# Query norms moved into the softmax's scale and the delta rule's output norm, in a two-block transformer kernel

## The chip, the cores and the metric
One core of one Trainium2 chip runs the whole program in one launch. The metric is the device time in microseconds. Three timed runs of the kernel before gave 3331.95, 3326.08 and 3330.05 us, median 3330.05. TensorE (PE) multiplies, VectorE (DVE), ScalarE (ACT) and GpSimd (POOL) work elementwise, SyncE (SP) issues the transfers.

## The reference
Two transformer blocks over 512 tokens of width 1024, in fp32. Block one is a SwiGLU layer, three mixers in parallel (retention, differential attention, attention to a memory of 256 rows) and a second SwiGLU layer. Block two is a gated delta rule beside an mLSTM, a feed-forward layer, a sliding-window attention and a second feed-forward layer. What the change touches:

```python
# differential attention: 8 heads, two maps each, width 64
dq = _rope_partial(_rms(dq.reshape(B, S, DIFF_HEADS, 2, DIFF_DK), diff_q_norm[l]), d_cos, d_sin)
dk = _rope_partial(_rms(dk.reshape(B, S, DIFF_HEADS, 2, DIFF_DK), diff_k_norm[l]), d_cos, d_sin)
s = einsum('bhrqd,bhrkd->bhrqk', q, k) / sqrt(DIFF_DK);  p = softmax(s);  a = p[0] - lam * p[1]
# memory attention: 4 heads, width 256
mq = _rms(mq.reshape(B, S, MEM_HEADS, MEM_DH), mem_q_norm[l])
mk = _rms(mk.reshape(B, M, MEM_HEADS, MEM_DH), mem_k_norm[l])
p = softmax(einsum('bshd,bmhd->bhsm', mq, mk) / sqrt(MEM_DH))
# delta rule: 4 heads, width 128; its output is linear in q
qa = l2norm(silu(conv(...))) * (A_DK ** -0.5);  ka = l2norm(silu(conv(...)))
oa = rmsnorm(gated_delta_rule(qa, ka, va, g, beta), norm_a) * silu(z)
```

## The kernel before, in words
Activations lie transposed in SBUF, channels on the 128 partitions, the 512 tokens along the free side. All weights come in 1002 panels of four 128x128 blocks. SyncE loads a panel into RAW, ScalarE rounds it to the fp32r tile WH, POOL subtracts (WL = RAW - WH). A product of a block is three matmuls, high x high, low x high and high x low (`mm3`, called by `lin` and `row_of`), each 128x512.

The program is one list of steps, `PLAN`, built by `plan_ffn`, `plan_ret`, `plan_diff`, `plan_mem`, `plan_ab`, `plan_swa` and `plan_feed`. Each engine's function walks the same list from front to back and issues, for every step, its own part (`tensor`, `vector`, `scalar`, `gpsimd`, `sync`), with semaphore waits (`at`) for what the others produce (`up`). So the order on every engine is the order of the list, and an instruction that waits holds back everything behind it on its engine. At each step ScalarE and POOL first convert the weight panels that are due (`starts`), at most six ahead. A PSUM bank is handed out by `bank`, which takes the one whose last content is consumed at the earliest step.

A norm has these parts. ScalarE squares. TensorE sums over the partitions with a column of ones (`columns`, products of one column). VectorE adds epsilon (`variance`), POOL takes the power -1/2 (`power`), VectorE sharpens it with three small operations (`factor`; `pre` is a further scaling). Since the tokens lie along the free side, TensorE must spread the factor: `spread` transposes a broadcast column with four 128x128 transposes (`turned`, line 548), and VectorE multiplies the tile by the result in PSUM.

Differential attention, head h, while head n = h+1 is prepared: `d_q(n,0)` and `d_q(n,1)` compute q and k, `d_v(n)` v, the sums for the norms of q and k (four columns) and their factor. VectorE copies the factors to two wide tiles (line 1312), `d_n(n)` turns them, four transposes for q and four for k, and VectorE multiplies. `d_rope` rotates: a matmul with a swap matrix, VectorE times sine, POOL times cosine, VectorE adds both. `d_sc(h,q)` is the scores of query block q (VectorE: mask, maximum, times -1/8; ScalarE: Exp with scale 1/8), `d_sm(h,q)` the division and the difference, `d_turn(h,q)` the transposes of the result on TensorE, `d_pv` the product with v, `d_t1` and `d_t2` the head's output norm. In the list, `d_q(n,0)` stands ahead of `d_sm(h,0)` and `d_turn(h,0)`, and `d_v(n)` ahead of `d_sm(h,3)` and `d_turn(h,3)`. `wide` products (gates, the retention's output, memory queries) fill the places between.

Memory attention: `mq(m)` queries, `mkl`/`mk` keys, `nqm` and `nkm` their norms, `mqn(h)` and `mkn(h)` the spreading, `ms` the scores and softmax, `mt` the transposes.

Delta rule, heads in two pairs: `c(h,j)` the convolution of q, k, v and Silu, `f(h)` the norms of q and k in one go (two columns), `n(h)` spread and multiply both, `dec` the decays, `LT` and `at` the products with k and q, `l` the seven levels of a triangular inverse, `uw`, `s` and `o` the recurrence and output, `z` the gate and the output norm's sum and factor, `fin` its spreading. The mLSTM's steps (`m_*`) lie in between.

Of the kernel before, what the change touches and what calls it, by code (L numbers as in the profile page):

```python
# [11 lines left out]
ACT = mybir.ActivationFunctionType  # L12
AX = mybir.AxisListType.X

T = 512
# [108 lines left out]
VOFF = {}  # L124
# [88 lines left out]
def plan_diff():  # L213
# [3 lines left out]
    p = [("d_q", 0, 0), ("d_q", 0, 1), ("d_v", 0), ("d_vt", 0), wide.pop(0), ("d_n", 0), wide.pop(0), ("d_rope", 0, 0), ("d_rope", 0, 1),  # L217
# [17 lines left out]
def plan_mem():  # L235
    p = [("mload",)] + [("mg", 1, m) for m in range(8)]
    p += [("mp", m) for m in range(5)] + [("mq", 6)] + [("mp", m) for m in (5, 6, 7)] + [("mq", 7)]
    p += [("mkl", 0), ("nqm",), ("fac", "nmem"), ("mkl", 1), ("bc", "nmem"), ("mk", 0), ("mk", 1), ("mqn", 0)]
    for m in range(2, 8):
        p += [("mkl", m), ("mk", m)] + ([("mqn", m // 2)] if m % 2 else [])  # L240
# [113 lines left out]
PLAN = plan()  # L354
# [9 lines left out]
def program(nc, x_in, mem_in, p_in, pos1, pos2, lam_in, vec_in, cst_in, dm_in, wst, out, total, dry=False):  # L364
    blocks = []
    with ExitStack() as ctx:
# [57 lines left out]
        for h_ in range(4):  # L424
            NORM["nr", h_] = ("b", 1 / 512, 4, 4, 1, 1.0)
            NORM["nqk", h_] = ("e", 1.0, 2, 4, 2, 1.0)
            NORM["no", h_] = ("e", 1 / 128, 1, 4, 1, 1.0)
            NORM["nml", h_] = ("e", 1 / 128, 1, 4, 1, 1.0)
# [12 lines left out]
        def nr(n):  # L441
            return nw(n)[:, 3, :].rearrange("p (t c) -> p t c", t=NORM[n][3])

# [13 lines left out]
        def tensor(e):  # L457
# [103 lines left out]
            for marks.step, (kind, *i) in enumerate(PLAN):  # L561
# [92 lines left out]
                elif kind == "d_v":  # L654
                    h = i[0]
                    lin(("d_v", h), ("d_v", h), "w_in", 0, cc(O_DV + 128 * h), range(8))
                    o = bank("var", ("nd", h))
# [8 lines left out]
                elif kind == "d_n":  # L666
                    h = i[0]
                    for j in range(2):
                        e.wait_ge(*at("d_wide", h, j))
                        turned(("d_normed", h, j), ("d_n", h, j), lambda t: quarter(tmp(2 + j), t))  # L670
                elif kind == "d_rope":
                    h, j = i
                    o = bank("d_sin", h, j)
                    e.wait_ge(*at("d_normed", h, j))
                    mm(o, CST[:, C_SWD:C_SWD + 128], ar(2 * (h % 2) + j), True, True).then_inc(*up("mm", "d_rope", h, j))
                elif kind == "d_sc":
                    h, q = i
                    nk = 128 * (q + 1)
                    for r in range(2):
                        o, lo = bank("d_exp", h, q, r), 64 * r  # L680
                        if q == 0 and r == 0:
                            e.wait_ge(*at("d_roped", h, 1))
# [56 lines left out]
                elif kind == "mqn":  # L739
                    spread("nqm", ("mq_normed", i[0], 1), ("mqn", i[0]), i[0])  # L740
# [7 lines left out]
                elif kind == "ms":  # L748
                    h, q = i
                    o = bank("ms_exp", h, q)[:, 0:256]  # L750
                    if q == 0:
                        e.wait_ge(*at("mk_normed", h, 1))
# [62 lines left out]
                elif kind == "f":  # L815
                    h = i[0]
                    o = bank("var", ("nqk", h))
                    e.wait_ge(*at("c_square", h, 1))
                    columns(o, 0, tmp(2), one1, True)
                    columns(o, 1, tmp(3), one1, False).then_inc(*up("mm", "fac", ("nqk", h)))  # L820
                elif kind == "n":
                    for j in range(2):
                        spread(("nqk", i[0]), ("qk_normed", i[0], j), ("n", i[0], j), j)
# [8 lines left out]
                elif kind == "LT":  # L832
                    h = i[0]
                    o = bank("kk", h)
                    e.wait_ge(*at("qk_normed", h, 1))
                    for t in range(4):
                        z = mm(quarter(o, t), quarter(slot(h, "k"), t), quarter(slot(h, "k"), t), True, True)
                    z.then_inc(*up("mm", "kk", h))
                    turned(("LT", h), ("beta", h), lambda t: SC[:, 0, 4 * t + h:4 * t + h + 1].to_broadcast([128, 128]))
                elif kind == "at":  # L840
                    h = i[0]
                    o = bank("att", h)
                    for t in range(4):
                        z = mm(quarter(o, t), quarter(slot(h, "k"), t), quarter(slot(h, "q"), t), True, True)
                    z.then_inc(*up("mm", "kq", h))
                    turned(("kd", h), ("k_turned", h), lambda t: quarter(slot(h, "k"), t))
                    e.wait_ge(*at("c_act", h, 2))
                    turned(("vb", h), ("v_turned", h), lambda t: quarter(slot(h, "v"), t))
                elif kind == "l":
# [12 lines left out]
                    else:  # L862
                        e.wait_ge(*at("l_x", h, lv))
                        e.wait_ge(*at("U", h, lv - 1))
                        if lv < 6:
                            o = bank("T", h, lv)
                            for t in range(4):
                                z = mm(quarter(o, t), quarter(U_, t), quarter(X_, t), True, True)
# [1554 lines left out]
```

## Time and profile before

| | |
|---|---|
| timed runs | 3326.08, 3330.05, 3331.95 us |
| profiled execution, its own time | 3324.88 us |
| its span (first to last instruction) | 3323.1 us |
| mean granted TensorE clock | 0.986 |
| VectorE busy | 1214.4 us (37%), 2152 instructions |
| ScalarE busy | 1230.6 us (37%), 2217 |
| POOL busy | 1743.3 us (52%), 1347 |

Busy time counts an engine's instructions in the span. A matmul's end is modelled, so back-to-back matmuls overlap. The differential attention lies between about 772 and 1160 us, the memory attention between 1160 and 1330, the delta rule and mLSTM between 1836 and 2210.

### The profile page before, as it was taken

The page shows a single profiled execution, that of the slowest core. Times are in us where ns is not written, and L with a number is a line of the kernel's source. Part 1 is how long each engine was busy: PE and PEld are TensorE (multiplying, and loading weights), DVE is VectorE, ACT ScalarE, POOL GpSimd, SP SyncE. Part 2 cuts the span into 40 slices and gives each one's busy share as a digit, 9 for nine tenths or more (in the row PEclk, how much of TensorE's full clock was granted, in tenths as well). Part 3 has the DMA queues.
Part 4 walks back from the last instruction along what each step waited for, and adds up shares of the span by engine and source line. Part 5 has one row for each costly group of instructions (what it writes and reads, how often), then busy time and mean ns, then how long its engine had stood idle before and what let it go on. Part 6 is the DMA issues. An engine that isn't in the chain of part 4 may idle for free.

```text
span 3323.1 us, 40114 instructions
## 1 busy us (share of the span) xinstructions
PE 3203.2 (96%) x15078; PEld 2612.8 (79%) x15078; DVE 1214.4 (37%) x2152; ACT 1230.6 (37%) x2217; POOL 1743.3 (52%) x1347
## 2 busy tenths in 40 slices
PE   8999999999999999999999898999999988999999
PEld 7888887777777787788888787877888776778887
DVE  4222322124555434223224655524111457341115
ACT  4332333333444435333224323234333345543333
POOL 6555655455554464465556213246555652475555
PEclk9999999999999999999999999999999999999999
DMA  4333222222222233333333102112333321223332
GB/s 163 98 92 101 86 86 76 83 82 77 64 61 61 70 106 97 88 98 98 98 96 95 54 26 58 39 54 80 101 96 95 96 70 39 64 85 100 96 101 86
DMA packets 149839, 275.58 MB, mean 83 GB/s; under 512 B 16528, under 2 KB 17808, under 8 KB 149520
## 3 DMA queue, kind: packets, MB, share of 16 engines
q1 hardware_dynamic: 149648, 273.02, 28.2%
q8 instruction: 122, 2.00, 0.2%
q14 instruction: 69, 0.57, 0.1%
HBM read 270.86 MB, written 2.10 MB: 82 GB/s over the span
## 4 chain that ended last, share of the span: by engine, by line
PE 85%; DVE 9%; POOL 3%; ACT 2%; issue 2%; DMA 0%; DVEq 0%; SPq 0%; ACTq 0%; POOLq 0%
PE PS L481 83%; PE PS L548 2%; POOL SM L2180 1%; DVE AR L1070 1%; POOL WL L2180 1%; DVE TMP L1070 1%; DVE ACC L1076 1%; DVE X L1070 1%; DVE AL L1070 1%; DVE HL L1076 1%; ACT AR L1795 1%; DVE SM L1070 1%; DVE TMP L1076 1%; DVE SM L1755 1%; DVE AR L1076 1%
## 5 line engine op out<-in xcount | busy, mean ns | idle before, releaser
L2180 POOL TENSOR_TENSOR WL<-RAW,WH 128x512 fp32r<-128x512 f32 x1002 | 1305.2, 1314 | 995.0 <-ACT WH L1795 994.2
L1795 ACT ACTIVATE WH<-RAW 128x512 fp32r<-128x512 f32 x1002 | 619.1, 627 | 1068.6 <-PE PS L481 1015.7
L481 PE MATMUL PS<-HH,WH 128*128 128x512 f32 x2296 | 914.0, 398 | 10.4 <-ACT WH L1795 7.1
L481 PE MATMUL PS<-HL,WH 128*128 128x512 f32 x2296 | 902.3, 393 | 7.9 <-DVE HL L1076 6.3
L481 PE MATMUL PS<-HH,WL 128*128 128x512 f32 x2296 | 901.5, 393 | 2.3 <-POOL WL L2180 2.3
L481 PE MATMUL PS<-AH,WH 128*128 128x512 f32 (+1 forms) x1504 | 584.3, 388 | 5.1 <-ACT AH L1795 3.5
L481 PE MATMUL PS<-AL,WH 128*128 128x512 f32 (+1 forms) x1504 | 582.1, 387 | 1.7 <-DVE AL L1070 1.1
L481 PE MATMUL PS<-AH,WL 128*128 128x512 f32 (+1 forms) x1504 | 580.9, 386 | 2.0 <-POOL WL L2180 2.0
L481 PEld LDWEIGHTS PS<-HL,WH 128*128 128x128 f32 x2296 | 435.7, 190 | 104.0 <-DVE HL L1076 12.1
L481 PEld LDWEIGHTS PS<-HH,WH 128*128 128x128 f32 x2296 | 435.3, 190 | 103.9 <-ACT WH L1795 7.4
L481 PEld LDWEIGHTS PS<-HH,WL 128*128 128x128 f32 x2296 | 434.8, 189 | 95.9 <-POOL WL L2180 4.2
L481 PEld LDWEIGHTS PS<-AL,WH 128*128 128x128 f32 x1504 | 284.2, 189 | 64.0 <-DVE AL L1070 7.9
L481 PEld LDWEIGHTS PS<-AH,WH 128*128 128x128 f32 x1504 | 284.2, 189 | 63.5 <-issue 5.5
L481 PEld LDWEIGHTS PS<-AH,WL 128*128 128x128 f32 x1504 | 284.2, 189 | 58.6 <-POOL WL L2180 2.8
L2180 POOL TENSOR_TENSOR AL<-TMP,AH 128x512 fp32r<-128x512 f32 x132 | 175.7, 1338 | 231.1 <-ACT AH L1795 231.1
L1070 DVE TENSOR_TENSOR TMP<-PS,RBT 128x512 f32<-128x512 f32 x141 | 96.8, 690 | 492.9 <-PE PS L481 487.7
L481 PE MATMUL PS<-AR 128*128 128x128 f32 (+8 forms) x1304 | 238.2, 359 | 17.0 <-DVE AR L1070 8.7
L481 PEld LDWEIGHTS PS<-AR 128*128 128x128 f32 (+2 forms) x1304 | 171.2, 192 | 74.1 <-issue 49.0
L1070 DVE TENSOR_TENSOR ACC<-ACC,PS 128x512 f32<-128x512 f32 x136 | 93.4, 687 | 266.3 <-PE PS L481 266.3
L2180 POOL TENSOR_TENSOR TMP<-TMP 128x512 f32<-128x512 f32 (+1 forms) x88 | 119.6, 1359 | 90.6 <-ACT TMP L1795 89.3
L2180 POOL TENSOR_TENSOR SM<-SM,VC 128x4 f32<-128x4 f32 (+3 forms) x47 | 67.4, 1433 | 178.0 <-DVE SM L1073 178.0
L1795 ACT ACTIVATE TMP<-TMP 128x512 f32<-128x512 f32 x132 | 82.7, 626 | 179.3 <-DVE TMP L1076 133.9
(208 smaller groups left out, 2576.0 us busy)
## 6 DMA issues: line engine op xcount, KB each, us to landing
RAW<-in_wst SPq DMA_DIRECT2D x1002, 256.0 KB, 2.6
X<-in_x SPq DMA_DIRECT2D x8, 256.0 KB, 5.0
TMP<-in_p SPq DMA_DIRECT2D x8, 256.0 KB, 3.2
out<-X SPq DMA_DIRECT2D x8, 256.0 KB, 2.0
AR<-in_dm SPq DMA_DIRECT2D x1, 1024.0 KB, 5.3
AR<-in_mem SPq DMA_DIRECT2D x1, 1024.0 KB, 5.8
CST<-in_cst SPq DMA_DIRECT2D x1, 964.0 KB, 7.6
AR<-in_pos SPq DMA_DIRECT2D x2, 256.0 KB, 2.9
```

The source lines that it names most:

```text
L481: return e.matmul(o, l, r, start=a, stop=z, skip_group_check=True)
L548: z = e.transpose(quarter(o, t), src(t), ident)
L1070: return e.tensor_tensor(o, a, b, op)
L1076: return e.scalar_tensor_tensor(out=o, in0=a, scalar=s, in1=b, op0=op0, op1=op1)
L1755: e.reduce_max(st[:, 0, :], p, AX).then_inc(*up("s_max", n))
L1795: return e.activation(o, a, f, **kw)
L2180: return e.tensor_tensor(o, a, b, op)
```

## The change
- Differential attention: q is no longer multiplied by its factor. The gain alone is multiplied in (`d_gain`, directly behind `d_q(n,0)`, after the square), and the factor times 1/8 (`eighth`) becomes Exp's scale and the maximum's multiplier. `d_n` spreads k only. The rotation's sine part stays in PSUM and is added from there.
- Memory attention: `mqn` goes. The factor of q times 1/16 (`mem_scale`) becomes the softmax's scale; the two gains are multiplied and applied to the keys.
- Delta rule: q stays as it is. Its factor times 128^-0.5 (`q_scale`) enters the output norm twice, in the variance and in the factor. The joint norm of q and k becomes two, `fk` and `fq`, one after the other.
- `split` cuts the steps of the list into finer ones, and `turns` gives an engine its own order by a table of shifts, `LATE`, which is empty.
- `d_rope(0,0)` of the first head moves ahead of a wide product and of `d_n(0)`.

```diff
-    p = [("d_q", 0, 0), ("d_q", 0, 1), ("d_v", 0), ("d_vt", 0), wide.pop(0), ("d_n", 0), wide.pop(0), ("d_rope", 0, 0), ("d_rope", 0, 1),
+    p = [("d_q", 0, 0), ("d_q", 0, 1), ("d_v", 0), ("d_vt", 0), ("d_rope", 0, 0), wide.pop(0), ("d_n", 0), wide.pop(0), ("d_rope", 0, 1),
...
-        p += [("mkl", m), ("mk", m)] + ([("mqn", m // 2)] if m % 2 else [])
+        p += [("mkl", m), ("mk", m)]
...
-PLAN = plan()
+def split(steps):
+
+    out = []
+    for s in steps:
+        kind, *i = s
+        h = i[0] if i else None
+        if kind == "fac":
+            out += [s, ("x", h)]
+        elif kind in ("nqm", "nkm"):
+            out += [s, ("x", kind)]
+        elif kind == "d_v":
+            out += [s, ("d_f", h), ("x", ("nd", h)), ("d_wide", h)]
+        elif kind == "d_q" and i[1] == 0:
+            out += [s, ("d_gain", h)]
+        elif kind == "f":
+            out += [("fk", h), ("x", ("nk", h)), ("fq", h), ("x", ("nq", h))]
...
+        elif kind == "z":
+            out += [s, ("zf", h), ("x", ("no", h))]
...
+        elif kind == "d_rope":
+            out += [s, ("d_add", *i)]
...
+PLAN = split(plan())
+LATE = {"vector": {}, "scalar": {}, "gpsimd": {}}
+
+
+def turns(engine):
+
+
+    place = {s: n + LATE[engine][s] + math.copysign(0.5, LATE[engine][s]) if s in LATE[engine] else n for n, s in enumerate(PLAN)}
+    return sorted((p, n, s) for n, (s, p) in enumerate(place.items()))
...
# TensorE
-                    for j in range(2):
-                        e.wait_ge(*at("d_wide", h, j))
-                        turned(("d_normed", h, j), ("d_n", h, j), lambda t: quarter(tmp(2 + j), t))
+                    e.wait_ge(*at("d_wide", h))
+                    turned(("d_normed", h), ("d_n", h), lambda t: quarter(tmp(3), t))
...
-                elif kind == "mqn":
-                    spread("nqm", ("mq_normed", i[0], 1), ("mqn", i[0]), i[0])
...
-                    e.wait_ge(*at("c_square", h, 1))
-                    columns(o, 0, tmp(2), one1, True)
-                    columns(o, 1, tmp(3), one1, False).then_inc(*up("mm", "fac", ("nqk", h)))
+                elif kind in ("fk", "fq"):
+                    n = ("n" + kind[1], i[0])
+                    o = bank("var", n)
+                    e.wait_ge(*at("c_square", i[0], int(kind == "fk")))
+                    columns(o, 0, tmp(2 + int(kind == "fk")), one1, True).then_inc(*up("mm", "fac", n))
                 elif kind == "n":
-                    for j in range(2):
-                        spread(("nqk", i[0]), ("qk_normed", i[0], j), ("n", i[0], j), j)
+                    spread(("nk", i[0]), ("k_normed", i[0]), ("n", i[0]))
...
# VectorE
+                    if n == "nqm":
+                        e.wait_ge(*at("factor", n))
+                        ts(mem_scale, nr(n), 0.0625, None, MUL).then_inc(*up("mem_scale"))
+                    elif n[0] == "nq":
+                        e.wait_ge(*at("factor", n))
+                        ts(q_scale(n[1]), nr(n), 128.0 ** -0.5, None, MUL).then_inc(*up("q_scale", n[1]))
...
-                    for j in range(2):
-                        src = nr(("nd", h))[:, :, 2 * j:2 * j + 2].unsqueeze(3).to_broadcast([128, 4, 2, 64])
-                        e.tensor_copy(tmp(2 + j).rearrange("p (a b c) -> p a b c", a=4, b=2), src).then_inc(*up("d_wide", h, j))
+                    src = nr(("nd", h))[:, :, 2:4].unsqueeze(3).to_broadcast([128, 4, 2, 64])
+                    e.tensor_copy(tmp(3).rearrange("p (a b c) -> p a b c", a=4, b=2), src).then_inc(*up("d_wide", h))
+                    ts(eighth(h), nr(("nd", h))[:, :, 0:2], 0.125, None, MUL).then_inc(*up("d_eighth", h))
+                elif kind == "d_gain":
+                    q = ar(2 * (i[0] % 2))
+                    e.wait_ge(*at("d_square", i[0], 0))
+                    ts(q, q, vcol("dq"), None, MUL).then_inc(*up("d_gain", i[0]))
...
-                    tt(r, psum("d_sin", h, j), tab(3), MUL).then_inc(*up("d_sin", h, j))
+                    tt(r, r, tab(3), MUL).then_inc(*up("d_sin", h, j))
+                elif kind == "d_add":
+                    h, j = i
+                    q, r, s = tmp(2 + j), psum("d_roped", h, j), ar(2 * (h % 2) + j)
...
-                    ts(st[:, 1:2], st[:, 0:1], -0.0625, None, MUL).then_inc(*up("ms_neg", h, q))
+                    e.wait_ge(*at("mem_scale"))
+                    stt(st[:, 1:2], st[:, 0:1], -1.0, mem_scale[:, q, h:h + 1], MUL, MUL).then_inc(*up("ms_neg", h, q))
...
-                    for j, p in enumerate(("q", "k")):
-                        e.wait_ge(*at("mm", "n", h, j))
-                        e.wait_ge(*at("c_square", h, j))
-                        stt(slot(h, p), slot(h, p), (128.0 ** -0.5, 1.0)[j], psum("qk_normed", h, j), MUL,
-                            MUL).then_inc(*up("qk_normed", h, j))
+                    o = slot(h, "k")
+                    e.wait_ge(*at("mm", "n", h))
+                    e.wait_ge(*at("c_square", h, 1))
+                    tt(o, o, psum("k_normed", h), MUL).then_inc(*up("k_normed", h))
...
-                    variance(("no", h))
-                    factor(("no", h))
+                elif kind == "zf":
+                    e.wait_ge(*at("q_scale", i[0]))
+                    scaled_variance(("no", i[0]), q_scale(i[0]))
...
# ScalarE
-                        act(ar(16 + 2 * (q % 2) + r)[:, 0:nk], psum("d_exp", h, q, r)[:, 0:nk], ACT.Exp, st[:, 2 + r:3 + r], 0.125,
-                            st[:, 4 + r:5 + r]).then_inc(*up("d_exp", h, q, r))
+                        act(ar(16 + 2 * (q % 2) + r)[:, 0:nk], psum("d_exp", h, q, r)[:, 0:nk], ACT.Exp, st[:, 2 + r:3 + r],
+                            eighth(h)[:, q, r:r + 1], st[:, 4 + r:5 + r]).then_inc(*up("d_exp", h, q, r))
```

## Rows read from the trace of the kernel before

**Rows 1.** The page: busy us (share of the span) x instructions of each engine
```profile
PE 3203.2 (96%) x15078; PEld 2612.8 (79%) x15078; DVE 1214.4 (37%) x2152; ACT 1230.6 (37%) x2217; POOL 1743.3 (52%) x1347
```
**Rows 2.** Groups by line and shape: busy us, mean ns, idle before and its releasers
```profile
L548 PE MATMUL PS<-CST,TMP 128*128 128x128 f32 x128 | 18.4, 276 | 0.5 <-DVE TMP L1312 0.5
```
**Rows 3.** Who waited for whom: us in total, times, longest us
```profile
PE PS L548 <- DVE AR L1076: 15.6, 12, 2.1
```
**Rows 4.** Timeline, PE, head 0: start us, us, instruction, count, idle before
```profile
832.42 1.04 PE L548 MATMUL PS<-CST,TMP 128*128 128x128 f32 x8
834.60 2.39 PE L481 MATMUL PS<-AR 128*128 128x512 f32 x8 [1.14 <-ACT AR L1795]
```
**Rows 5.** Timeline of four engines around d_turn of head 6, block 0
```profile
1079.08 0.69 DVE L1070 TENSOR_TENSOR AR<-PS,RBT 128x512 f32<-128x512 f32 x1 [2.11 <-PE PS L481]
1080.01 0.75 DVE L1073 TENSOR_SCALAR AR<-AR,SM 128x128 f32<-128x128 f32 x1
...
1079.80 0.63 ACT L1795 ACTIVATE TMP<-AR 128x512 f32<-128x512 f32 x1 [1.20 <-DVE AR L1070]
...
1078.17 2.51 POOL L2180 TENSOR_TENSOR WL<-RAW,WH 128x512 fp32r<-128x512 f32 x2 [3.50 <-ACT WH L1795]
...
1081.28 0.33 PE L548 MATMUL PS<-CST,AR 128*128 128x128 f32 x1 [0.96 <-DVE AR L1076]
```
**Rows 6.** Timeline, VectorE and PE around d_turn of head 6, block 3
```profile
1101.67 0.76 DVE L1312 COPY TMP<-SM 128x512 f32<-128x512 f32 x2
1102.67 0.48 DVE L1073 TENSOR_SCALAR AR<-AR,SM 128x512 f32<-128x512 f32 x1
...
1104.07 0.66 PE L548 MATMUL PS<-CST,AR 128*128 128x128 f32 x4 [2.07 <-DVE AR L1076]
```
**Rows 7.** Timeline, VectorE and PE at the rotation of head 1
```profile
840.08 1.51 DVE L1070 TENSOR_TENSOR AR<-TMP 128x512 f32<-128x512 f32 x1
...
841.74 0.49 PE L481 MATMUL PS<-AR 64*128 64x128 f32 x4 [0.30 <-DVE AR L1070]
```
**Rows 8.** Timeline, PE, d_n of the first head
```profile
789.38 1.09 PE L548 MATMUL PS<-CST,TMP 128*128 128x128 f32 x8 [0.46 <-DVE TMP L1312]
```
**Rows 9.** Timeline: PE in the memory attention; an activation with a tile's bias
```profile
1235.03 1.34 PE L548 MATMUL PS<-CST,SM 128*128 128x128 f32 x6 [3.03 <-DVE SM L1076]
...
1284.80 0.44 PE L548 MATMUL PS<-CST,AR 128*128 128x128 f32 x2 [0.27 <-DVE AR L1073]
...
1072.11 0.72 ACT L1795 ACTIVATE AR<-AR,VC 128x512 f32<-128x512 f32 x1 [2.53 <-DVE AR L1070]
```
**Rows 10.** Timeline at the norms of delta rule heads 0 and 1
```profile
1829.40 1.01 POOL L2180 TENSOR_TENSOR SM<-SM,VC 128x4 f32<-128x4 f32 x1 [2.83 <-DVE SM L1073]
1864.87 1.63 POOL L2180 TENSOR_TENSOR SM<-SM,VC 128x8 f32<-128x8 f32 x1 [5.88 <-DVE SM L1073]
...
1866.74 2.40 DVE L1076 SCALAR_TENSOR_TENSOR SM<-SM 128x8 f32<-128x8 f32 x2
...
1869.19 1.97 PE L548 MATMUL PS<-CST,SM 128*128 128x128 f32 x8 [5.77 <-DVE SM L1076]
...
1911.90 2.05 PE L481 MATMUL PS<-AR,TMP 128*128 128x128 f32 x8 [2.96 <-DVE TMP L1070]
```
**Rows 11.** Timeline, PE at heads 2 and 3; the group of VectorE's short products
```profile
2029.86 0.49 PE L481 MATMUL PS<-AR 128*128 128x128 f32 x2 [2.91 <-DVE AR L1070]
...
2047.66 1.94 PE L548 MATMUL PS<-CST,SM 128*128 128x128 f32 x8 [4.39 <-issue]
...
L1076 DVE SCALAR_TENSOR_TENSOR SM<-SM 128x4 f32<-128x4 f32 x68 | 15.3, 225 | 2.3
```
**Rows 12.** Busy us (x) of PE, PEld, DVE, ACT, POOL by stretch; then PE's clock, DMA
```profile
770.00:1200.00 430.00, 408.70 (x1963) 317.79 (x1962) 215.41 (x522) 179.15 (x360) 223.65 (x166) 1.00 0.24 71
...
1866.80:1873.50 6.70, 4.31 (x14) 3.76 (x15) 5.89 (x9) 1.09 (x3) 2.31 (x2) 0.50 0.29 78
...
2044.30:2051.00 6.70, 3.34 (x16) 3.37 (x17) 2.82 (x8) 0.63 (x1) 1.63 (x1) 0.50 0.00 0
```

More of the change, by code:

```diff
@@ L442, in nr, with eighth, q_scale @@
             return nw(n)[:, 3, :].rearrange("p (t c) -> p t c", t=NORM[n][3])
+        mem_gain = small("c", "mem_gain", 2)
+        mem_scale = small("c", "mem_scale", 16).rearrange("p (t c) -> p t c", t=4)
+        def eighth(h):
+            return small("b", ("d_eighth", h % 2), 8).rearrange("p (t c) -> p t c", t=4)
+        def q_scale(h):
+            return small("e", ("q_scale", h), 4).rearrange("p (t c) -> p t c", c=1)
         def sq(n, k):
@@ L1036, in tensor @@
                 elif kind == "st":
-                    n = i[0]
+                    n, q = i
                     e.wait_ge(*at("s_p", n))
-                    for q in range(2):
-                        turned(("s_turned", n, q), ("st", n, q), lambda t: s_p(n)[:, 2 * q + t // 2, 128 * (t % 2):128 * (t % 2) + 128])
+                    turned(("s_turned", n, q), ("st", n, q), lambda t: s_p(n)[:, 2 * q + t // 2, 128 * (t % 2):128 * (t % 2) + 128])
                 elif kind == "sp":
@@ L1138, in vector @@
             e.wait_ge(*at("vec"))
-            for marks.step, (kind, *i) in enumerate(PLAN):
+            for marks.step, _, (kind, *i) in turns("vector"):
                 if kind == "fac":
@@ L1264, in vector @@
                     variance(("nr", i[0]))
-                    factor(("nr", i[0]))
                 elif kind == "r_fin":
@@ L1356, in vector @@
                     variance(("nt", i[0]))
-                    factor(("nt", i[0]))
                 elif kind == "d_t2":
@@ L1656, in vector @@
                     scaled_variance(("nml", i[0]), dn[:, 0])
-                    factor(("nml", i[0]), dn[:, 0])
                 elif kind == "m_fin":
@@ L1808, in scalar @@
             e.wait_ge(*at("vec"))
-            for s, (kind, *i) in enumerate(PLAN):
-                marks.step = s
+            for marks.step, s, (kind, *i) in turns("scalar"):
                 if kind == "f_open" and i[0] == 0:
@@ L2196, in gpsimd @@
             e.wait_ge(*at("vec"))
-            for s, (kind, *i) in enumerate(PLAN):
-                marks.step = s
+            for marks.step, s, (kind, *i) in turns("gpsimd"):
                 while panels < starts(s):
@@ L2242, in gpsimd @@
                     h, j = i
-                    e.wait_ge(*at("d_normed", h, j))
-                    e.wait_ge(*(at("mm", "fac", ("nd", h)) if j == 0 else at("mm", "d_n", h, 1)))
+                    e.wait_ge(*at(("d_gain", "d_normed")[j], h))
+                    if j == 0 and h:
+                        e.wait_ge(*at("d_roped", h - 1, 0))
                     if h == 0 and j == 0:
                         e.wait_ge(*at("table", 0, 3))
-                    tt(tmp(4 - 2 * j), ar(2 * (h % 2) + j), tab(2), MUL).then_inc(*up("d_cos", h, j))
+                    tt(tmp(2 + j), ar(2 * (h % 2) + j), tab(2), MUL).then_inc(*up("d_cos", h, j))
                 elif kind == "d_t2":
```

179 lines of the change are left out of this document (114 added, 65 removed).

## The prediction

> **What bounds the kernel now.** The page's busy line comes first: TensorE (PE) is busy for 3203.2 of 3323.1 us [rows 1]. So an instruction removed on another engine is worth nothing by itself. The time moves when TensorE issues less, or when it waits less. The groups by line say what it issues: product passes of the weight panels, which the change doesn't touch, and small transposes, of which it removes some (L548 is `turned`; 128 of them read TMP) [rows 2]. The list of waits says where TensorE stands: the largest entry is transposes that wait for a VectorE result in AR, 15.6 us in 12 waits [rows 3]. The reader is to see that the idle time, 120 us, is made of pieces of 0.3 to 6 us with different releasers, so each edit is priced at its own piece, in the timeline.
>
> **The sum is made against the profiled execution**, 3324.9 us, span 3323.1 and 1.8 around it. It is 5.2 us under the median of the three timed runs, 3330.05; the sum's difference is added to that median.
>
> **Transposes removed.** Eight in a row take 1.04 us [rows 4], the last one 0.28 [rows 2]: (1.04 - 0.28) / 7 = 0.11 us each. The differential attention loses 4 in each of 8 heads (`d_n` of q), the memory attention 16 (`mqn`), the delta rule 4 in each of 4 heads (`n` of q): 32 x 0.11 = -3.5, 16 x 0.11 = -1.8, and 16 whose worth is taken up below, since they stand beside waits.
>
> **Given back at once.** In heads 0, 2 and 4 `d_pv` follows `d_n` directly and already waits for ScalarE's copy of the last turned block, 1.14 us at 834.60 [rows 4]. Four transposes fewer is 0.44 us more waiting, 3 x 0.44 = +1.3.
>
> **The new gain instruction, the dearest edit.** `d_gain(n)` comes behind `d_q(n,0)` on VectorE, waits there for ScalarE's square of the same tile, and multiplies 128x512 in place. Queued behind it on VectorE is `d_sm(h,0)`, and TensorE's `d_turn(h,0)` waits for that already, 0.96 us at 1081.28 [rows 5]. There is no cover. `d_q`'s product runs from 1079.08 to 1079.77, the square from 1079.80 to 1080.43, POOL's subtraction until 1080.68 [rows 5], so the gain starts near 1080.5 and takes 0.48 us, as the scalar product of 128x512 at 1102.67 did [rows 6]. `d_sm`'s first step, which began as `d_q`'s product ended, begins near 1081.1, 1.4 us late. Part comes back: its 128x128 product at 1080.01 took 0.75 us, more than the larger one at 1102.67, because POOL was at work [rows 5, 6]; now it runs after POOL is done. Worked through, the probabilities are late by 0.93 us here and in three heads like it, 1.0 in two where that product was slowed less, and 1.25 in head 0, where it was not slowed: 7 heads (the eighth issues no next query), +7.0. Bounds: the bare 0.48 each, +3.4, if the square were always there; no return at all, 1.4 each, +9.8. I take +7.0, as the order on the three engines is the same in all heads.
>
> **The rest of this section.** `d_turn(h,3)` waits 2.07 us in heads 1, 3, 5 and 6 for a VectorE queue that holds the factor and two wide copies (0.76 us for both) [rows 6]; one copy goes (-0.34) and a product of 8 columns comes (0.1 to 0.2): 4 x -0.2 = -0.8. The rotation's sum now reads PSUM and one SBUF tile, not two SBUF tiles. At 840.08 it took 1.51 us, and `d_sc` waited 0.30 us for it at 841.74 [rows 7]; a sum or product with a PSUM operand takes 0.69 (1079.08) [rows 5]. 2 heads x -0.3 = -0.6; in the others wide products cover it. The Trainium skill, "SBUF — State Buffer", section on who interferes with whom, has an exclusive lock between VectorE and GpSimd, which a VectorE instruction with two SBUF inputs or in a two-port mode contends for; the trace agrees at 1080.01 and 840.08, and the rule also speaks against the change, for the gain is such an instruction: where it met a whole POOL instruction it would cost up to 1.3 us more. In head 0 the move of `d_rope(0,0)` ahead of `d_n(0)` puts a rotation's matmul in front of a 0.46 us wait (789.38) [rows 8]: -0.6 with the pipeline's refill. No DMA moves, and no weight panel: the new steps consume none, so the order of conversions is kept on ScalarE, POOL and SP. Sum: -3.5 +1.3 +7.0 -0.8 -0.6 -0.6 = +2.8.
>
> **Memory attention.** -1.8 from the transposes. The wait of 3.03 us at 1235.03 stands behind two factors in a row on VectorE [rows 9]; the new `mem_scale` comes between them, +0.3. The softmax is a ring over TensorE, VectorE and ScalarE with no slack: a wait of 0.27 us already stands before its first transpose, at 1284.80 [rows 9]. An Exp with its scale read from a tile is shown nowhere; the nearest rows are an activation with a bias from a tile, 0.72 us, and one without, 0.63 [rows 5, 9], so 0 to 0.1 per step; the bias here comes from a tile already, so I take 0.03, 16 x 0.03 = +0.5 (0 to +1.6). Sum -1.0.
>
> **Delta rule.** The key's norm and the query's norm are now two roundtrips to POOL, and VectorE is blocked in both.
> - Heads 0, 1: `n(0)` stands 5.77 us for the factor at 1869.19. The key's factor alone comes near 1866.6: POOL 1.01 us for four columns (1829.40) in place of 1.63 for eight (1864.87), and three short products [rows 10]. That releases TensorE 2.5 us earlier. But VectorE is next late: it holds back the following convolution until the query's factor is done too, and POOL starts its weight subtraction right behind the power, where two short products took 2.40 us (1866.74) [rows 10]. I get 1870.4 for that convolution, +1.3, and +1.2 behind the second pair, less 2 x 0.6 for the product of q that goes and the slack VectorE had between. The wait at 1911.90, 2.96 us for VectorE [rows 10], hands this on: -0.3 in all, from -2.5 (all the earliness stays) to +1.5.
> - Head 2: TensorE waits until 2029.86 for a VectorE sum queued behind the factor [rows 11]: the second roundtrip adds 1.5. Head 3: it waits 4.39 us, until 2047.66, for the factor itself; that comes 0.65 earlier, and four of eight transposes (1.94 us) go [rows 11]: -1.6.
> - Output norm of head 3: two instructions more in front of the power and one behind it, 0.2 each as a short product has [rows 11], and nothing but four transposes beside them: +0.6.
> Sum +0.2.
>
> **Total** +2.8 -1.0 +0.2 = +2.0: 3326.9 for an execution like the profiled one, 3332.1 as a median. The finer steps move nothing by themselves: they issue the same instructions in the same order on each engine, since the table of shifts is empty.
>
> **Rivals.**
> 1. *The delta rule gives back speed too (faster).* From 1867 to 1873.5 TensorE has the lower clock, 0.50 or 1.2 GHz, around the long wait, and again from 2044.3 to 2051 [rows 12]. If the shorter waits at 1869 and 2047 leave the clock at 2.4 GHz, 4.3 and 3.3 us of work (busy in these rows) shrink by half, -2.2 and -1.7; with the 2.5 us at 1869 kept, 1.6 at 2047, 0.9 of transposes in heads 1 and 2, against +0.6, that is -8.3, and with the other two sections 3323.6. For it: the lower clock stands around such waits. Against: the wait at 1911.90 shows VectorE late there anyway.
> 2. *The longer waits in the attention drop the clock (slower).* At `d_turn(h,0)` there are transposes, short products and 0.96 us of wait together, and the wait doubles. The clock is 1.00 from 770 to 1200, with the four 2.07 us waits in it [rows 12]. A stretch as long as the one at 1867, were it full of work, costs 3.3. One fall changes nothing that could be told; from two on, +2.0 +6.6, it is slower: 3338.7, and 3345 with four. The Trainium skill, "TensorE: Matmul & The Clock Gate", Part 1, says that idleness halves the clock; by that rule the falls at 1867 and 2044 are no surprise, but the 2.07 us waits passed without one.
> 3. *The change costs nothing where I see its price*: the gain is hidden, +7.0 becomes 0, and 3325.1 results. Against it: 0.03 us lie between the product and the square that waits for it [rows 5].
>
> **Chances.** Forecast 0.58, rival 1 0.16, rival 2 0.15, rival 3 0.06, and 0.05 for what no row shows. About 0.2% (6.7 us) is what a measurement of this kernel can tell from no change. Of the forecast and of rival 3 nearly all lies within it; rival 1 lies just at its edge. Faster 0.22, same 0.58, slower 0.20. The range of 8 in 10, with the bounds of the gain (-3.6, +2.8) and of heads 0 and 1 (-2.2, +1.8) and most of rivals 1 and 2 in it: 3321 to 3341.
>
> **What would show it.** Right: `d_turn(h,0)` waits 1.8 to 2.2 us in seven heads and as before in the eighth, VectorE idle for ScalarE ahead of each gain; 64 records of L548 fewer; 2.07 at `d_turn(h,3)` down to 1.9; the wait before `n(0)` near 3 us and a larger one at 1911.90; the clock 1.00 throughout the attention. Wrong: unchanged waits at `d_turn(h,0)` (rival 3), stretches at 0.50 in the attention (rival 2), fewer of them from 1850 to 2060 with no larger wait at 1911.90 (rival 1), or a wait for a PSUM bank.

## The result, and the profile after

The changed kernel takes 3338.89 us (median of 8 runs, 3335.62 to 3341.14) against 3331.11 us of the kernel before (8 runs, 3326.08 to 3338.12): ratio 1.0023, 95% interval 1.0014 to 1.0032. The forecast was 3332.1, +2.0; measured is +7.8 us, 0.23%. The interval, 0.14 to 0.32%, leaves out no change at all and has the prediction's bound of 0.2% inside: the kernel is slower, by about as much as the forecast still called the same. The profiled execution took 3338.05 us, with a span of 3336.3 and a mean granted clock of 0.983. It stands 0.8 under its kernel's median, while the one of before (3324.88) stands 6.2 under its own. So a comparison of the two traces shows 13.2 us, and about 5 of them belong to the pair of executions and not to the change.

TensorE (PE) has 64 records fewer than in [rows 1] and is no less busy. Of the transposes that read TMP, 32 are gone ([rows 2] had 128). The wait that the prediction was about, [rows 3] with 15.6 us, has grown. The page's busy line, a group by line and shape (busy us, mean ns, idle before), and an entry of the list of waits (us in total, times, longest) of the kernel after:

```profile
PE 3205.2 (96%) x15014; PEld 2612.2 (78%) x15014; DVE 1216.1 (36%) x2174; ACT 1237.6 (37%) x2217; POOL 1745.4 (52%) x1351
...
L610 PE MATMUL PS<-CST,TMP 128*128 128x128 f32 x96 | 14.9, 278 | 1.0 <-DVE TMP L1398 0.7 <-DVE TMP L1142 0.3
...
PE PS L610 <- DVE AR L1148: 22.6, 12, 2.5
```

The timeline of the kernel after, first around `d_turn` of head 6, block 0, which answers to [rows 5], then the same place in head 1 (start us, us, engine, instruction, in brackets the idle time before it):

```profile
1086.30 0.69 DVE L1142 TENSOR_TENSOR AR<-PS,RBT 128x512 f32<-128x512 f32 x1 [2.08 <-PE PS L543]
1087.69 0.61 DVE L1145 TENSOR_SCALAR AR<-AR,VC 128x512 f32<-128x512 f32 x1 [0.70 <-ACT TMP L1894]
...
1087.03 0.63 ACT L1894 ACTIVATE TMP<-AR 128x512 f32<-128x512 f32 x1 [1.07 <-DVE AR L1142]
...
1085.52 2.50 POOL L2277 TENSOR_TENSOR WL<-RAW,WH 128x512 fp32r<-128x512 f32 x2 [3.61 <-ACT WH L1894]
...
1089.34 0.33 PE L610 MATMUL PS<-CST,AR 128*128 128x128 f32 x1 [1.80 <-DVE AR L1148]
...
850.21 2.49 POOL L2277 TENSOR_TENSOR WL<-RAW,WH 128x512 fp32r<-128x512 f32 x2 [3.60 <-ACT WH L1894]
...
851.69 1.29 DVE L1145 TENSOR_SCALAR AR<-AR,VC 128x512 f32<-128x512 f32 x1 [0.70 <-ACT TMP L1894]
...
854.02 0.47 PE L610 MATMUL PS<-CST,AR 128*128 128x128 f32 x1 [2.47 <-DVE AR L1148]
```

The reader is to see the chain as predicted: product, 0.70 us idle for ScalarE's square, gain, probabilities, transpose. TensorE waits 1.80 us in head 6 where it waited 0.96 [rows 5]. In heads 1 and 3 the gain starts when most of a POOL instruction is still to come, takes 1.29 us instead of 0.61, and the wait is 2.47. In both heads shown it ends 0.28 us behind POOL's last instruction (852.98 for 852.70, 1088.30 for 1088.02). The seven waits add up to 14.2 us, against 6.3 before; the eighth (1.08) is nearly as it was.

The second thing to see is new. The same stretch as in [rows 12], and five us of it (us, then busy us (count) of PE, PEld, DVE, ACT, POOL; granted clock, DMA share, GB/s):

```profile
770.00:1200.00 430.00, 401.25 (x1893) 310.60 (x1892) 215.43 (x521) 183.07 (x357) 218.38 (x163) 0.99 0.24 69
853.00:858.00 5.00, 3.98 (x11) 3.22 (x12) 4.67 (x14) 1.71 (x4) 1.28 (x1) 0.66 0.30 95
```

There were no half-clock stretches in the attention of the profiled execution before. Now there are three, from 854, 946 and 1090 us, each at a `d_turn(h,0)` whose wait was 2.47, 2.47 and 1.80 us.

TensorE at the delta rule's norms, which answers to [rows 10, 11], and at the last output norm:

```profile
1878.61 1.11 PE L610 MATMUL PS<-CST,SM 128*128 128x128 f32 x4 [3.10 <-DVE SM L1148]
...
1924.70 1.62 PE L543 MATMUL PS<-AR,TMP 128*128 128x128 f32 x6 [3.81 <-DVE TMP L1142]
...
2043.05 0.79 PE L543 MATMUL PS<-AR 128*128 128x128 f32 x2 [4.22 <-DVE AR L1142]
...
2060.93 1.09 PE L610 MATMUL PS<-CST,SM 128*128 128x128 f32 x4 [3.75 <-issue]
...
2219.35 1.12 PE L610 MATMUL PS<-CST,SM 128*128 128x128 f32 x4 [2.11 <-DVE SM L1142]
```

Instruction for instruction, the lag of the kernel after behind the kernel before was read off at places that both have: 0.4 us at the start of the attention, 9.1 at its end, 8.9 behind the memory attention's ring, 10.5 from 1410 on, 10.5 again at the start of the delta rule, 10.8 behind it (at 2313), 13.2 at the end. The attention takes 8.7 of it.

### The profile page after: what moved, and what is told of

The parts are those of the page before. It is cut to its first block, busy times and chain, and to the rows that moved or that the text cites. A ratio compares the mean times of both kernels' runs of the same rounds, so it can differ in the third digit from the quotient of the medians.

```text
span 3336.3 us, 40115 instructions
## 1 busy us (share of the span) xinstructions
PE 3205.2 (96%) x15014; PEld 2612.2 (78%) x15014; DVE 1216.1 (36%) x2174; ACT 1237.6 (37%) x2217; POOL 1745.4 (52%) x1351
## 4 chain that ended last, share of the span: by engine, by line
PE 84%; DVE 9%; POOL 3%; ACT 2%; issue 2%; DMA 0%; DVEq 0%; SPq 0%; ACTq 0%; POOLq 0%
PE PS L543 83%; PE PS L610 1%; POOL WL L2277 1%; DVE AR L1142 1%; POOL SM L2277 1%; DVE TMP L1142 1%; DVE TMP L1148 1%; DVE ACC L1148 1%; DVE SM L1142 1%; DVE HL L1148 1%; DVE AL L1142 1%; ACT AR L1894 1%; DVE X L1142 1%; DVE SM L1148 1%; POOL TMP L2277 0%
```

## The experiments

All were timed in five rounds beside the kernel before. The changed kernel wasn't among them, so differences to it are between medians of different rounds, and the ratios to the kernel before are the safer comparison. Lines of a diff are against the changed kernel, or against the kernel named.

**The gain, later.** The steps' finer parts let one engine take a part out of turn, through the table of shifts:

```
+for h in range(7):
+    LATE["vector"]["d_gain", h + 1] = PLAN.index(("d_sm", h, 1)) - PLAN.index(("d_gain", h + 1))
```

> VectorE does the gain of the next head's queries behind the probabilities of blocks 0 and 1, where it stood idle for about 1 us, not between the product of d_q and the probabilities. Theory A (the gain in front of the probabilities lengthens TensorE's wait at d_turn(h,0), and these longer waits make the clock fall): the seven waits there go from 1.8 to 2.5 back to 0.75 to 0.97 us (-8.0 us in all), the three half-clock stretches of the attention (854, 946, 1090) go, about 1.7 us each (-5): 3326 us, 5 under the kernel before. Theory B (the waits are the gain's, the falls of the clock are not): -8 alone, 3331. Theory C (the gain only moves to another place on the path, in front of the product of d_q(n,1)): d_turn(h,1) or d_sc(h,3) waits 0.5 us or more in its place, and the time stays at 3336 to 3339.

Measured: 3327.38 us, ratio 0.9988 (0.9979 to 0.9997), 11.5 us under the changed kernel and, by the interval, a little under the kernel before. The attention's row and head 6 of this kernel:

```profile
770.00:1200.00 430.00, 407.23 (x1940) 315.97 (x1939) 219.96 (x525) 185.34 (x362) 224.62 (x167) 1.00 0.25 71
...
1076.19 0.56 ACT L1896 ACTIVATE AR<-PS,SM 128x256 f32<-128x256 f32 x1 [1.08 <-DVE SM L1150]
...
1079.96 0.87 DVE L1147 TENSOR_SCALAR AR<-AR,SM 128x128 f32<-128x128 f32 x1
...
1081.35 0.33 PE L612 MATMUL PS<-CST,AR 128*128 128x128 f32 x1 [1.08 <-DVE AR L1150]
```

Theory C falls: no wait elsewhere grew. Theory A's place and total hold, but its first number missed. The seven waits sum to 8.3 us, not to the 6.3 of before, so the gain's own share is 14.2 - 8.3 = 5.9, and 2.0 has another cause. The rest of the 11.5 us, 5.6, is more than any wait of this trace returns, and the attention's three half-clock stretches are gone. The clocks of the timed executions say the same of more than one trace. One minus the mean granted clock (recorded in thousandths for each execution), times the time, is what the lower clock withheld: on average 57.2 us in the kernel after and 49.9 here, each good to about 1 us. It is a bound of what the clock cost, for it counts the time in which TensorE waited too. The difference, 7.3, and the rest, 4.2, agree with 5.6 and 5.9 to within 2 us.

**The gain, left out.** The step and its waits go, and the rotation reads the queries as they are.

> Leaves out the multiplication of the queries by their gain in the differential attention; nothing else differs from the changed kernel. It is the floor for any place of this instruction. Theory A: 3325 to 3326 us, within 1 us of the kernel with the late gain. Theory B: 3331. If the late gain costs something where it stands (theory C), this one is faster than that by that cost, 3 to 10 us.

Measured: 3327.65 us, 0.9992 (0.9983 to 1.0001). Moved late, the instruction costs nothing; the 2.0 us are still there (waits of 1.07 to 1.48 us), so they aren't the gain's.

**The wait, filled.** Work is laid into TensorE's wait, and nothing comes sooner:

```
+                    if q == 0 and h < 7:
+                        for _ in range(6):
+                            mm(o, HH[:, 0, 0:128], HH[:, 0, :], True, True)
                     e.wait_ge(*at("d_p", h, q))
```

> The changed kernel with six wide products of 512 columns (1.3 us by the 0.21 us of a product pass) put on TensorE into the bank of d_turn(h,0), in heads 0 to 6, ahead of the wait of 1.8 to 2.5 us for the probabilities; their result is overwritten. The probabilities come no earlier, so the wait that is left is 0.5 to 1.2 us and the end of it stays. Theory A (idle TensorE makes the clock fall here): granted clock 1.00 from 770 to 1200 us, no half-clock stretch near 854, 946 and 1090, and 5 us less than the changed kernel: 3334 us. Rival (the falls come by chance of the run or from the kind of work and not from the wait): the same three or other stretches at 0.50, and 3339 to 3341 us.

Measured: 3335.62 us, 1.0018 (1.0009 to 1.0027). That is 3.3 under the changed kernel by the medians and 1.7 by the ratios, whose intervals overlap, and no probability comes sooner. TensorE in head 1 (two rows) and the granted clock from 876 us:

```profile
855.38 0.33 PE L757 MATMUL PS<-CST,AR 128*128 128x128 f32 x1 [0.92 <-DVE AR L1154]
...
878.09 1.03 PE L757 MATMUL PS<-CST,AR 128*128 128x128 f32 x4 [1.98 <-DVE AR L1154]
...
876.00:881.00 5.00, 3.02 (x12) 0.72 0.27 76
```

None of the seven filled waits has a half-clock stretch. That speaks for theory A, and so do the clocks of the timed executions (55.2 us withheld, for 57.2). But the clock wasn't 1.00 throughout, as theory A had it: it fell twice at `d_turn(h,3)`, whose wait of 1.9 to 2.0 us was left as it was. The rival allowed for other stretches and missed the time. None in seven against three in seven is little, and the gain in time lies within the noise: this run makes the clock's part likely and doesn't prove it.

**The attention's part undone.** Both wide copies, eight transposes and the constant scale are back, the gain instruction is gone, and `d_rope(0,0)` stands where it stood. The rotation's sum still reads PSUM; the rest of the change stays.

> The differential attention's query norm as before (two wide copies, eight transposes, the scale constant, no gain instruction of its own); memory attention, delta rule and finer steps as in the changed kernel. If the whole loss is the attention's, as the aligned traces say (+8.7 us of the gap stands in front of the memory attention), the time is 3330 us, at or up to 1.5 us under the kernel before. If the delta rule or the finer steps lose too (part of the gap is added behind 1310 us in the two profiles, +1.6 at 1410 and +1.3 towards the end), it is 3333 to 3335.

Measured: 3331.24 us, 1.0001 (0.9992 to 1.0010). The loss, 1.0023 against 1.0001, is the attention's: 7.3 us. Its trace has two half-clock stretches in the attention, at waits of 2.07 us that the kernel before had at the same places with the clock at 1.00. One is at head 6 [rows 6], the other, shown here, at head 5:

```profile
1055.24 1.12 PE L610 MATMUL PS<-CST,AR 128*128 128x128 f32 x4 [2.07 <-DVE AR L1149]
...
1054.00:1060.00 6.00, 4.76 (x20) 0.72 0.12 42
```

**The scale of Exp, constant.** On the kernel with the late gain:

```
-ACT.Exp, st[:, 2 + r:3 + r], eighth(h)[:, q, r:r + 1], ...
+ACT.Exp, st[:, 2 + r:3 + r], 0.125, ...
-ACT.Exp, st[:, 1:2], mem_scale[:, q, h:h + 1], ...
+ACT.Exp, st[:, 1:2], 0.0625, ...
```

The bias's multiplier goes back to a constant as well (not shown), so this kernel leaves the queries' factor out of the softmax.

> The late gain, and both attentions' Exp with a constant scale as before: leaves out the queries' factor in the softmax (it is still computed). Theory A (an Exp with its scale from a tile is 0.09 us longer, and this is paid on the path): the Exp of 128x128, 128x256 and 128x384 go from 0.46, 0.56 and 0.67 us back to 0.37, 0.47 and 0.58; in the memory attention the ring's pitch goes from 1.80 to 1.71, 16 x 0.09 = -1.4; in the differential attention the conversion behind two Exps comes 0.08 earlier, so POOL's subtraction does too, the product beside it is shorter, and the waits at d_turn(h,0) go from 1.07 to 1.36 down to 0.75 to 0.97, -0.3 in each of 7 heads, -2.0: in all 3.4 us under the late gain's 3327.4, 3324. Rival (the product of three operands that makes the bias, or something else, is the cost): the pitch stays 1.80 or the waits stay above 1.0, 3326 to 3327.5.

Measured: 3325.18 us, 0.9981 (0.9972 to 0.9989), 2.2 under the late gain, between the two expectations and with overlapping intervals; the durations and waits decide. First the memory attention's ring in the kernel after, an Exp and a transpose, then the same two here, and head 6's product and transpose here:

```profile
1295.75 0.56 ACT L1894 ACTIVATE AR<-PS,SM 128x256 f32<-128x256 f32 x1 [1.15 <-DVE SM L1148]
...
1297.05 0.44 PE L610 MATMUL PS<-CST,AR 128*128 128x128 f32 x2 [0.50 <-DVE AR L1145]
```

```profile
1284.31 0.47 ACT L1896 ACTIVATE AR<-PS,SM 128x256 f32<-128x256 f32 x1 [1.14 <-DVE SM L1147]
...
1283.81 0.44 PE L612 MATMUL PS<-CST,AR 128*128 128x128 f32 x2 [0.40 <-DVE AR L1147]
...
1079.60 0.74 DVE L1147 TENSOR_SCALAR AR<-AR,SM 128x128 f32<-128x128 f32 x1
...
1080.86 0.33 PE L612 MATMUL PS<-CST,AR 128*128 128x128 f32 x1 [0.94 <-DVE AR L1150]
```

Each Exp is 0.09 us longer with a scale from a tile, and theory A holds for both paths: the waits at `d_turn(h,0)` sum to 6.6 us (from 8.3), and the ring's wait falls by 0.10. That is 3.3 us of waits; this trace has one half-clock stretch in the attention, at 876 us, that the late gain's has not. The path in the attention is a roundabout one. Two longer Exps delay ScalarE's conversion of a panel by 0.08, with it POOL's subtraction, and the VectorE product beside that takes 0.87 instead of 0.74. The Trainium skill, "ScalarE: Activation LUTs", section "What ACT_TABLE_LOAD costs", adds about 93 ns for each operand of an ACTIVATE that is a pointer to a column; these rows agree.

**The rest of the queries' factor, late.** On the kernel with the late gain, in the delta rule:

```
+for h, behind in enumerate((("m_v", 1), ("m_v", 1), ("s", 0, 3, 0), ("s", 1, 3, 1))):
+    LATE["vector"]["fq", h] = -1
+    LATE["vector"]["x", ("nq", h)] = PLAN.index(behind) - PLAN.index(("x", ("nq", h)))
```

> The late gain, and in the delta rule VectorE does the variance of the queries beside that of the keys, while the rest of the queries' factor comes only where VectorE was idle for 4 to 7 us. Theory A (the second roundtrip to POOL holds VectorE on the path): the wait of 3.81 us at 1913 goes back to 3 or less, that of 4.22 at 2032 to 2.9 or less, while those of 2.63 at 1867 and 3.75 at 2050 stay: -0.9 -1.4 and something at 2036, 3325 us. Rival (POOL's second power delays its weight subtraction and so the same VectorE products, whoever waits for the factor, or TensorE waits for another operand): the waits at 1913 and 2032 stay within 0.3 us, 3327 to 3328.

Measured: 3319.96 us, 0.9967 (0.9955 to 0.9979); run again beside other kernels it was 3320.35, 0.9971 (0.9960 to 0.9982). VectorE at head 0's norms, and TensorE's wait that was 3.81 us:

```profile
1865.82 0.22 DVE L1150 TENSOR_SCALAR SM<-PS 128x4 f32<-128x4 f32 x2
1867.10 0.16 DVE L1147 TENSOR_TENSOR SM<-SM 128x4 f32<-128x4 f32 x1 [1.05 <-POOL SM L2282]
1867.30 0.36 DVE L1153 SCALAR_TENSOR_TENSOR SM<-SM 128x4 f32<-128x4 f32 x2
1867.57 0.69 DVE L1147 TENSOR_TENSOR TMP<-PS,RBT 128x512 f32<-128x512 f32 x1
...
1909.47 2.05 PE L548 MATMUL PS<-AR,TMP 128*128 128x128 f32 x8 [3.34 <-DVE TMP L1147]
```

The same place of VectorE in the kernel after:

```profile
1878.19 0.36 DVE L1148 SCALAR_TENSOR_TENSOR SM<-SM 128x4 f32<-128x4 f32 x2
...
1879.74 1.23 DVE L1142 TENSOR_TENSOR SM<-SM 128x4 f32<-128x4 f32 x1 [1.12 <-POOL SM L2277]
1881.01 1.40 DVE L1148 SCALAR_TENSOR_TENSOR SM<-SM 128x4 f32<-128x4 f32 x2
...
1882.52 0.69 DVE L1142 TENSOR_TENSOR TMP<-PS,RBT 128x512 f32<-128x512 f32 x1
```

Now VectorE goes from the keys' factor straight to the convolution at 1867.57. Before, 4.0 us lay between them (1878.55 to 1882.52): the queries' roundtrip, with its short products beside POOL's subtraction at 1.23 and 1.40 us. Theory A is right in its cause and too small in its sum: -7.4 us where -2.4 was expected. The wait of 3.81 gave 0.5, and smaller ones between 1890 and 1909 (1.8 us together) went. From 2024 to 2050 the waits fell from 10.15 us to 8.3, but not where I had said: 4.22 + 2.18 became 0.19 + 4.36. All waits between 1836 and 2060 together are 5.0 us shorter; the remaining 2 us aren't placed.

**The memory attention's part undone**, on the kernel with the late gain:

> The late gain, and the memory attention's query norm as before (16 transposes, constant scale). My sum had the memory's part at -1.0; the slower Exp, 16 x 0.09 = 1.4 instead of 0.5, makes it -0.1 to -0.5. Then this kernel is 0 to 0.5 us above the late gain's 3327.4. A half-clock stretch stands near 1403 to 1414 in every kernel with the changed memory attention and in the kernel before not (+1.6 between 1310 and 1410): if the changed ring causes it, it is absent here, the offset against before stays level from 1310 to 1410, and the time is 1.1 to 1.5 us lower, 3326.

Measured: 3327.74 us, 0.9993 (0.9984 to 1.0001), against 3327.38: no difference. The traces show two that cancel, 1.4 and 1.6 us. Between 1210 and 1310 us this kernel loses 0.8 against the kernel before, and the one with the late gain wins 0.6. Behind it, the changed memory attention has a stretch at half clock; rows of PE, of the kernel after and of this one:

```profile
1380.00:1430.00 50.00, 48.37 (x206) 0.97 0.30 85
```

```profile
1380.00:1430.00 50.00, 48.37 (x212) 1.00 0.31 90
```

**The delta rule's part undone**, on the same:

> The late gain, and the delta rule's norms as before (one factor of eight columns for queries and keys, eight transposes). Prediction's sum for this part: +0.2, so 3327.2. Waits at 1869 near 5.8, at 1912 near 3.0, at 2030 near 2.9, at 2048 near 4.4 as before. If the part costs more than the sum says (offsets of the changed and late kernels between 1860 and 2110: +0.7 to +2.9), 3325 to 3326; if it gains by a clock that falls less often, 3329 or more.

Measured: 3326.70 us, 0.9989 (0.9981 to 0.9998), against 0.9988. The waits are back to 5.80, 2.95, 2.90 and 4.39, as in [rows 10, 11]. The part is worth nothing in either direction, but it isn't without effect. In the timed executions the lower clock withheld 53.2 us here and 49.9 with the late gain, so the changed delta rule has some 3 us less under the lower clock and is no faster for it. Part of that shows in the traces, behind the places that rival 1 named; first this kernel, then the late gain (PE):

```profile
2110.00:2225.00 115.00, 109.58 (x652) 0.93 0.13 37
```

```profile
2110.00:2225.00 115.00, 108.69 (x661) 0.96 0.13 37
```

Why fewer stretches stand there, and where the gain is lost again, was not tried.

**Only the finer parts.** All three undone at once:

> All three query norms as before; of the change only the finer parts of the steps are left (and the rotation's sum that reads its sine product from PSUM). Theory A (finer steps issue the same instructions in the same order and cost nothing): 3330 us, ratio to the kernel before 1.000 within 0.001, waits at d_turn(h,0) 0.75 to 0.97, at 1869 5.8, at 2048 4.4. Rival (the added waits on semaphores between the parts, or TensorE's issue order, cost by themselves): 3332 to 3335, as part of the 1.2 us that the changed kernel without its attention part stood above the kernel before.

Measured: 3328.80 us, 0.9998 (0.9989 to 1.0007). Theory A: finer steps cost nothing by themselves.

**The late kernel again, and the recurrence first.** The repeat is the one named above:

> The kernel with the late gain and the late rest of the queries' factor in the delta rule, once more, beside the next two on one chip: 3320 us, ratio 0.997 to the kernel before, as in the run of 3319.96; if that run had luck, 3323 to 3325.

Its trace shows why 4.36 us of wait were left (VectorE, then TensorE, then 50 us of PE):

```profile
2023.45 0.68 DVE L1147 TENSOR_TENSOR TMP<-PS,RBT 128x512 f32<-128x512 f32 x1
2024.16 1.07 DVE L1150 TENSOR_SCALAR TMP<-TMP,VC 128x512 f32<-128x512 f32 x1
2025.27 3.20 DVE L1153 SCALAR_TENSOR_TENSOR TMP<-TMP,VC 128x511 f32<-128x511 f32 x3
2028.38 0.60 DVE L1153 SCALAR_TENSOR_TENSOR AR<-AR,SC,PS 128x128 f32<-128x128 f32 x2
...
2028.87 0.77 PE L548 MATMUL PS<-AR 128*128 128x128 f32 x2 [4.36 <-DVE AR L1153]
...
2042.62 1.09 PE L615 MATMUL PS<-CST,SM 128*128 128x128 f32 x4 [3.75 <-issue]
...
2005.00:2055.00 50.00, 41.71 (x210) 0.86 0.22 64
```

The states of the recurrence, 0.60 us, stand behind 5 us of convolution. One line more:

```
+LATE["vector"]["c", 3, 1] = 2
```

> The same, and VectorE does the convolution of head 3's keys (5 us of products) behind the two short state steps that the recurrence waits for, not ahead of them. In the trace of the late kernel TensorE waits 4.36 us at 2031 for a state that VectorE makes right behind this convolution. Theory A (the queue's order is that wait): it falls to about 1 us; the keys' factor comes 0.5 to 1 us later, so the wait of 3.75 at 2045 grows by as much: -2.5, 3317.5 us. Rival (the whole shift is handed to the next wait, because the factor needs the convolution anyway and TensorE has only one product between them): the two waits keep their sum of 8.1 us within 0.5, 3320.

Measured: 3314.78 us (3312.05 to 3317.81), 0.9957 (0.9945 to 0.9970), the fastest of all. The same three views:

```profile
2025.62 0.34 DVE L1154 SCALAR_TENSOR_TENSOR AR<-AR,SC,PS 128x128 f32<-128x128 f32 x1
2026.28 0.35 DVE L1154 SCALAR_TENSOR_TENSOR AR<-AR,SC,PS 128x128 f32<-128x128 f32 x1 [0.32 <-PE PS L549]
2026.55 0.68 DVE L1148 TENSOR_TENSOR TMP<-PS,RBT 128x512 f32<-128x512 f32 x1
...
2039.78 1.08 PE L616 MATMUL PS<-CST,SM 128*128 128x128 f32 x4 [5.37 <-issue]
...
2005.00:2055.00 50.00, 44.45 (x237) 0.93 0.22 64
```

The wait of 4.36 is gone, and the next grew by 1.6: -2.7, as theory A had it. The clock of the stretch rose from 0.86 to 0.93, because one of the two half-clock stretches there is gone. That is worth 0.07 x 50 = 3.5 us at most. In the timed executions the lower clock withheld 2.9 us less (46.4 for 49.3), and 2.7 + 2.9 is the 5.6 by which the medians differ. Every run of this kernel is faster than every run of the late kernel beside it.

**Late, with the old norm in the memory attention:**

> The late kernel with the memory attention's query norm as before. The shorter ring against the 16 transposes: +1.2 (offsets of the two late kernels between 1210 and 1310 us: +0.8 with the old norm, -0.4 with the new one), against the half-clock stretch near 1403 that only the new one has, -1.6: -0.4, 3319.6, so within 1 us of the run beside it. If the stretch comes in every execution and nothing is given back later it is 3319; if it was an accident of the profiled ones, 3321.

Measured: 3320.26 us, 0.9972 (0.9963 to 0.9982), beside 3320.35: equal again, and no stretch at half clock near 1403. The lower clock withheld 46.2 us here and 49.3 beside it, and 48.7 for 49.9 in the earlier pair: the new norm has more of it in both.

## Why the prediction was off by six microseconds

The direction and most places were right, the size wasn't: +7.8 us for a forecast of +2.0, with the time inside the range. Two steps of the prediction failed. The longer waits were given no price by the clock in the sum, and the scale from a tile was given none in the differential attention. By its own steps:

- **Differential attention, +2.8 forecast, 8.7 in the traces, 7.3 by undoing it (without the rotation's -0.6, which stayed).** Transposes: as counted, -3.5. `d_pv`: +0.8 (waits 1.32, 1.32, 1.24 for 1.14, 1.14, 0.81), not +1.3. The gain: +5.9, not +7.0; the mechanism is shown by moving it. It took longer than the 0.48 of the sum (0.61, and 1.29 in heads 1 and 3) and still cost less: 0.84 for 1.25 in head 0, 1.11 in heads 1 and 3 and 0.72 in the others for 0.93 to 1.0. `d_turn(h,3)`: 1.8 to 1.9 us for 2.07 to 2.15, -1.1, as said (-0.8). The rotation's sum: the waits of 0.30 are gone, -0.6. The move of `d_rope(0,0)`: no gain (forecast -0.6), since the wait behind it became 0.68. With the two terms below these make 8.3 of the 8.7 us.
- **A term that was missing: +2.0.** I priced Exp's scale from a tile in the memory attention alone, and at nothing in the differential one. It costs 0.09 us each, and reaches TensorE through ScalarE's queue and POOL. The constant scale returned 1.7 of the 2.0; the last 0.3 stand in the traces with the attention's part undone too (6.6 us for 6.3) and aren't its own.
- **A term that was given to a rival: +4.8 in the traces.** Three stretches at half clock at 1.6 us each (the lag jumps by so much at the one near 1410). As an average over the timed executions it is less sure: the lower clock withheld 57.2 us in the kernel after and 53.6 with the attention's part undone, a difference of 3.6, good to 1 us or so. The profiled execution before had none of these stretches, and that was luck: the two kernels whose attention is as before have two each in their traces. Rival 2 had the right mechanism with a chance of 0.15, a place that was right, and 3.3 us for a fall, twice too dear. That the 2.07 us waits "passed without one" was the reading that failed: it was made from one execution. In the 14 traces of this case the waits of 1.8 us and more in the attention number 63, and 13 of them have a stretch at half clock, 10 of 56 at `d_turn(h,3)` and 3 of 7 at the lengthened `d_turn(h,0)`. The shorter waits, to 1.6 us, have none.
- **Memory attention, -1.0 forecast, 0 by undoing it.** The Exps cost 16 x 0.09 = 1.4, not 0.5. That makes the sum -0.1, and the lag over this section fell by 0.1. The half-clock stretch at 1403 to 1414 added 1.6. Undoing finds nothing, and not 1.5, because the old norm's ring lost 0.8 us in its own trace against the same code in the kernel before, and the late gain's won 0.6: such differences between executions are as large as the effect.
- **Delta rule, +0.2 forecast; 0.3 in the traces, 0 by undoing it.** Waits forecast 3, larger than 2.96, +1.5, -0.65: measured 3.10, 3.81, +1.3, -0.64; the output norm of head 3, +0.6 forecast, 0.67 (2.11 for 1.44). Rival 1 is refuted at its places: the long wait at the first norm was halved and the half-clock stretches around it stayed. Less time is spent at the lower clock behind them, without making the kernel faster.
- **Rival 3**, the gain hidden, isn't this kernel's case, but it is what one shift makes of it.

What stays open: why the stretch near 1403 comes in all ten traces with the changed memory attention and in none of the four with the old one, although TensorE's waits there are the same (0.87 and 0.77 us). And the remainder behind 2313 us, whose code is the same in all, takes 2.4 to 2.8 us more than before in some traces and 0 to 0.3 in others, by where its half-clock stretches lie; nothing was tried on that.

## What to carry to other kernels

An instruction taken off the bounding engine is worth its time; one put into the queue of an engine that the bounding one already waits for costs its own time, the wait in front of it, and what the longer idle does to the clock. Before giving up such a change, look for the place in that queue where the engine is idle: here the same instruction went from 11.5 us to nothing, and short work of a recurrence put ahead of a long product that nobody needs yet brought 5.6 more. Price every operand that turns from a constant into a tile, in every place where it stands.

## What the runs showed of the hardware

- An ACTIVATE whose scale comes from a tile takes 0.09 us more than with a constant, at 128 (0.46 for 0.37), 256 (0.56 for 0.47) and 384 columns (0.67 for 0.58).
- At waits of some 2 us the granted clock fell in some executions and not in others: the same wait of 2.07 us left it at 1.00 in one kernel's execution and at 0.5 in another's, 13 of 63 waits of 1.8 to 2.5 us in all, and none of the shorter ones. The stretches of the attention cost about 1.6 us each.
- Filling seven waits of 1.8 to 2.5 us with matmuls that nobody needs brought 3.3 us by the medians and 1.7 by the ratios (not clear of noise), with nothing computed sooner; none of the seven had a half-clock stretch.
- A product of 128x512 on VectorE, from SBUF to SBUF, that starts beside POOL's subtraction ended 0.28 us behind the end of that subtraction, in each of the six heads where 0.3 us or more of it was left. So it took 0.61 us with 0.33 us left and 1.29 with 1.01 us left, against 0.48 in the kernel with the late gain, where the subtraction starts only as the product ends (857.97 + 0.48 and 858.44 in head 1).
